# Roots of means between projections: square root on ScalarE and reciprocal on VectorE for logarithm and exponential

## The chip, the cores and the metric

The kernel runs on one core of a Trainium2 chip. The metric is the device time of one execution in microseconds (us), as the median of several runs. TensorE (PE) multiplies matrices, VectorE (DVE), ScalarE (ACT) and GpSimd (POOL) work elementwise, SyncE (SP) issues the transfers.

## The reference, cut to what matters

A first transformer block is followed by a second block of two layers, all in float32, on 512 tokens of width 1024. The change touches the root-mean-square norms that stand between a projection and the next one:

```python
def rms_norm_2(x, g):
    xf = x.astype(jnp.float32)
    y = xf * lax.rsqrt(jnp.mean(xf * xf, axis=-1, keepdims=True) + EPS)
    return (y * g.astype(jnp.float32)).astype(x.dtype)

# second block, each layer l (two layers)
x = x + rms_norm_2(mix, mix_post_g[l])
h = rms_norm_2(x, mem_pre_g[l])
...
x = x + rms_norm_2(memory_cross_attention(h, mem_n, ...), mem_post_g[l])
h = rms_norm_2(x, ffn_pre_g[l])
x = x + rms_norm_2(conv_ffn_2(h, ...), ffn_post_g[l])
```

Between the two blocks, the first block's output is normed once (`norm_final`) and then normed again for the second block.

## The kernel before, in words

Activations lie transposed: 1024 features as 8 tiles (KT) of 128 partitions by 512 tokens. Weights come from memory in slabs of 128 x 2048 through a ring; ACT rounds each slab (L218) and DVE subtracts to get its lower part (L225), and every product is three matmuls (upper by upper, upper by lower, lower by upper). The program is a row of stages, each a block in which every engine has its own instruction list; at the end of a block all engines meet. The two layers of the second block are one hardware loop over the same stages.

A norm needs, for each token, the sum of squares over 1024 features. ACT squares the eight tiles, PE multiplies each by a matrix of ones and adds up in one bank, so that every partition holds the sum, and `root_of_mean` (L510 to L514) turns the 128 x 512 sums into scales: ACT takes the logarithm of mean plus epsilon (L512), drains, and takes the exponential of minus one half of it (L514). That is 1 / sqrt(mean + eps).

A **seam** is what follows a projection in the second block: class `PostNorm` (from L659). It has two roots. Three stages of a layer end with one: `mix_out` and `mem_out` (both `project`, L1475) and the down projection (`ffn_down`, L1405). In order:

- `square` (L683) and `sum` (L689) run while the projection's last tiles are computed. `rms` waits for the last sum and takes the **first root**, signalling `scale_ready`.
- ACT then rounds one slab (`round_second`). In `vector`, DVE waits for `scale_ready`, and for each tile multiplies by gain and scale (L732) and adds the result to the residual `xT` (L737, five tiles; POOL adds the other three, L746). Then DVE halves one slab (`halve_to`, L225).
- ACT squares the new `xT` tiles as they come (`next_squares`, L719), PE sums them (`next_sums`, L697), and `next_rms` takes the **second root**, for the norm with which the next stage begins. It signals nothing: the end of the block is what orders it before the next stage, whose DVE begins with the multiplication by that scale (L623 in `Norms`, with `given=True`).

`final_norm` (L2231), between the blocks, has the same two roots: the first is waited for by DVE (L2267), the second ends the stage. So the function is executed 3 x 2 x 2 + 2 = 14 times. Other norms (`Norms.scalar`, L581 and L583, and L2403 and L2405) have logarithm and exponential of their own.

ACT evaluates functions from a table; the compiler puts a table load (`ACT_TABLE_LOAD`) ahead of an activation whose function is not in the table that is loaded. The profile attributes it to the activation's line. The second block's other functions are the tanh form of GELU (L505 in `in2`, L1364 in the convolution) and the exponentials of softmax (L1077, L1220, L876).

Of the kernel before, what the change touches and what calls it, by code (L numbers as in the profile page):

```python
# [23 lines left out]
ACT = mybir.ActivationFunctionType  # L24
# [3 lines left out]
D = 1024  # L28
# [85 lines left out]
def build_program(nc, stream, xT_in, ctxT_in, memT_in, pos_in, const_in, axial_in, par1_in, par2_in, out):  # L114
    stack = ExitStack()
    with stack:
# [27 lines left out]
        bank = stack.enter_context(nc.psum_tensor("bank", [P, 8, 512], F32))  # L144
        post_gain = small[:, 0:KT]

        def con(name, n=P, at=0):
            return const[:, CONST[name] + at:CONST[name] + at + n]
# [156 lines left out]
        def stage(name, tensor=None, scalar=None, vector=None, gpsimd=None, sync=None):  # L305

            with nc.Block() as block:  # L307
                if tensor:
                    @block.tensor
                    def _(pe):  # L310
                        tensor(pe)

                @block.sync
                def _(sp):
                    if sync:
                        sync(sp)
                    ws.feed(sp, ws.limit)
                if scalar:
                    @block.scalar
                    def _(act):  # L320
                        scalar(act)
                if vector:
                    @block.vector
                    def _(dve):
                        vector(dve)
                if gpsimd:
                    @block.gpsimd
                    def _(pool):
                        gpsimd(pool)
# [179 lines left out]

        def root_of_mean(act, dst, sums):  # L510

            nc.scalar.activation(dst, sums, ACT.Ln, bias=con("eps", 1), scale=1.0 / D)  # L512
            act.drain()  # L513
            return nc.scalar.activation(dst, dst, ACT.Exp, scale=-0.5)  # L514

        class Norms:

# [123 lines left out]
            def gpsimd(self, pool):  # L641
                for k in range(1, 2 * self.halved, 2):
                    j = self.jobs[0]
                    pool.wait_ge(self.upper_ready.sem, self.upper_ready.at(k + 1))
                    nc.gpsimd.tensor_tensor(j["end"][2](k), j["out"](k), j["end"][1](k).bitcast(F32), ALU.subtract)\
                        .then_inc(self.lower_by_pool.sem, 1)
                for n, j in enumerate(self.jobs):
                    if j["end"] and j["end"][0] == "times":
                        for k in range(j["tiles"]):
                            pool.wait_ge(self.normed.sem, self.normed.at(self.starts[n] + k + 1))  # L650
                            nc.gpsimd.tensor_tensor(j["out"](k), j["end"][1](k), j["src"](k), ALU.mult)
# [7 lines left out]
        class PostNorm:  # L659
# [43 lines left out]

            def next_rms(self, act):
                act.wait_ge(self.next_square_summed.sem, self.next_square_summed.at(KT))
                root_of_mean(act, self.next_scale, bank[:, 1, :])

            def next_squares(self, act):
                pool = dve = 0
# [16 lines left out]

            def vector(self, dve, second):
                dve.wait_ge(self.scale_ready.sem, self.scale_ready.at(1))
                for n in range(KT + 1):
                    if n < KT:  # L730
                        src = bank[:, n, :] if n else self.raw[:, 0, :]
                        nc.vector.scalar_tensor_tensor(self.raw[:, n, :], src, self.gain(n), self.scale, ALU.mult, ALU.mult)\  # L732
                            .then_inc(self.normed.sem, 1)
                    if n >= 1 and n - 1 not in self.pool_tiles:

                        dve.wait_ge(self.normed.sem, self.normed.at(n))
                        nc.vector.tensor_tensor(xT[:, n - 1, :], xT[:, n - 1, :], self.raw[:, n - 1, :], ALU.add)\  # L737
                            .then_inc(self.added_by_dve.sem, 1)
                ws.halve_to(dve, second, second + 1)

            pool_tiles = range(0, KT, 3)

# [1025 lines left out]
        def tmp(name, shape, where=None, dt=F32):  # L1768
            return new(where or phase, name, shape, dt)
# [14 lines left out]
        with ExitStack() as here:  # L1784
# [15 lines left out]
            def sync(sp):  # L1800
                sp.dma_start(par1[:, :], par1_in).then_inc(params_in.sem, 16)
                ws.feed(sp, RING)
                sp.dma_start(const[:, :], const_in).then_inc(inputs_loaded.sem, 16)
                sp.dma_start(xT[:, :, :], xT_in).then_inc(inputs_loaded.sem, 16)
                sp.dma_start(pos_i[:, :], pos_in.to_broadcast([P, T])).then_inc(inputs_loaded.sem, 16)
# [21 lines left out]
            def tensor(pe):  # L1827

                def turn(g):
                    pe.wait_ge(rows_ready.sem, rows_ready.at(g + 1))  # L1830
                    for e in range(4):
                        n = 4 * g + e
                        last = nc.tensor.transpose(bank[:, 0, 2 * n:2 * n + 2], rows[:, n * P:(n + 1) * P], con("ident", 2)[0:2, :])
                    return last
                pe.wait_ge(c_ready.sem, c_ready.at(1))
                for g in range(GROUPS):
                    if g >= 4:
                        pe.wait_ge(rows_ready.sem, rows_ready.at(g - 3))
                    for k in range(KT):
                        b = B1_AT["mod"] + (g * KT + k) * 4  # L1840
                        last = ws.mm_whole(pe, b, bank[0:2, 1 + g % 4, :], sc[:, k, :], k == 0, k == KT - 1)
                    last.then_inc(group_done.sem, 1)
                    if g == 2:
                        pe.wait_ge(inputs_loaded.sem, 16 * 3)
                    if g >= 2:
                        turn(g - 2)
                turn(GROUPS - 2)
                turn(GROUPS - 1).then_inc(mod_done.sem, 1)
# [116 lines left out]
        with ExitStack() as s:  # L1965
# [8 lines left out]
            sums = [in_x[:, 0:C_HEADS * ALLT].rearrange("p (n t) -> p n t", n=C_HEADS), tmp("scan_sums", [P, C_HEADS, ALLT], s)]  # L1974
# [246 lines left out]
        scales2 = tmp("scales2", [P, 2, T], phase)  # L2221
# [9 lines left out]
        def final_norm():  # L2231

            squared = Signal("final_squared", 2 * KT)
            summed = Signal("final_summed", 2 * KT)
            normed = Signal("final_normed", KT)
            scale_ready = Signal("final_scale_ready", 1)
            params_loaded = Signal("params_loaded", 16)
            rows = squares2[:, 0:SQUARES, :]

            def sync(sp):  # L2240
                sp.dma_start(par2[:, :], par2_in[0]).then_inc(params_loaded.sem, 16)
                sp.wait_ge(params_loaded.sem, params_loaded.at(16))

            def scalar(act):
                for n in range(2 * KT):
                    if n >= SQUARES:
                        act.wait_ge(summed.sem, summed.at(n - SQUARES + 1))
                    if n >= KT:
                        act.wait_ge(normed.sem, normed.at(n - KT + 1))
                    nc.scalar.activation(rows[:, n % SQUARES, :], xT[:, n % KT, :], ACT.Square).then_inc(squared.sem, 1)  # L2250
                    if n == KT - 1:
                        act.wait_ge(summed.sem, summed.at(KT))
                        root_of_mean(act, scales2[:, 1, :], bank[:, 0, :]).then_inc(scale_ready.sem, 1)
                        ws.round_second(act, RING_SLABS + 1)
                act.wait_ge(summed.sem, summed.at(2 * KT))
                root_of_mean(act, scales2[:, 0, :], bank[:, 1, :])

            def tensor(pe):
                for n in range(2 * KT):
                    pe.wait_ge(squared.sem, squared.at(n + 1))  # L2260
                    nc.tensor.matmul(bank[:, n // KT, :], con("ones"), rows[:, n % SQUARES, :], start=n % KT == 0,
                                     stop=n % KT == KT - 1).then_inc(summed.sem, 1)

            def vector(dve):
                dve.wait_ge(scale_ready.sem, scale_ready.at(1))
                for n in range(KT):
                    nc.vector.scalar_tensor_tensor(xT[:, n, :], xT[:, n, :], p1("norm_final", 1, n), scales2[:, 1, :],  # L2267
                                                   ALU.mult, ALU.mult).then_inc(normed.sem, 1)
                ws.halve_to(dve, RING_SLABS + 1, RING_SLABS + 2)
            stage("norm_final", tensor=tensor, scalar=scalar, vector=vector, sync=sync)  # L2270
        final_norm()

# [427 lines left out]
```

## Time and profile before

| | us |
|---|---|
| median of 3 runs (lowest, highest) | 3588.16 (3587.02, 3592.61) |
| the profiled execution's own time | 3586.33 |
| its span, first to last instruction | 3584.5 |
| PE busy | 3089.6 (86%) |
| DVE busy | 1579.2 (44%) |
| ACT busy | 1337.3 (37%) |
| POOL busy | 555.9 (16%) |
| mean granted TensorE clock, as a share of full speed | 0.918 |

Busy time is the sum of an engine's instructions. PE is the busiest engine over the whole, which says nothing of single stretches: a seam has to be read in the timeline, where each row has its start, its duration, the engine, the line, the tensors and, in brackets, how long the engine had been idle and who ended that.

### The profile page before, as it was taken

What the parts mean: (1) busy time and instruction counts of PE and PEld (TensorE: products, weight loads), DVE (VectorE), ACT (ScalarE), POOL (GpSimd) and SP (SyncE); (2) the same over time, 40 slices, a digit from 0 to 9 for tenths busy, and PEclk for the clock granted to TensorE, in tenths of its full rate; (3) what the DMA queues carried; (4) which work ended last, traced back from release to release, by engine and by line L of the source; (5) the groups of instructions that cost most, each with busy time, mean ns of one, the idle gap of its engine ahead of it and who ended that gap; (6) DMA issues with size and microseconds to landing.
All of it is one profiled execution on the core that took longest, in us unless ns stands there. A gap on an engine that the chain in (4) does not pass through costs nothing. (4 is left out here: it accounts for less than half of the span.)

```text
span 3584.5 us, 40672 instructions
## 1 busy us (share of the span) xinstructions
PE 3089.6 (86%) x15048; PEld 2395.5 (67%) x15048; DVE 1579.2 (44%) x2077; ACT 1337.3 (37%) x1888; POOL 555.9 (16%) x519
## 2 busy tenths in 40 slices
PE   7886788779999999887878889999887788889998
PEld 2775766458877878664456768877664457768875
DVE  2455534336544443335634434442335643444433
ACT  3832224453233332433444333332433443343323
POOL 0144413230000110003301111100104210111100
PEclk8987989799999999998788999999998689999999
DMA  5100021004532222210012212222210022112222
GB/s 207 59 1 0 1 87 36 1 24 154 176 116 94 94 82 94 76 62 24 1 47 82 83 59 94 100 95 83 72 59 1 1 71 106 59 59 100 99 90 83
DMA packets 41485, 253.94 MB, mean 71 GB/s; under 512 B 4592, under 2 KB 4720, under 8 KB 13552
## 3 DMA queue, kind: packets, MB, share of 16 engines
q1 hardware_dynamic: 41328, 251.87, 19.6%
q8 instruction: 96, 1.57, 0.2%
q14 instruction: 61, 0.50, 0.0%
HBM read 249.75 MB, written 2.10 MB: 70 GB/s over the span
## 5 line engine op out<-in xcount | busy, mean ns | idle before, releaser
L225 DVE TENSOR_TENSOR ring_lo<-ring,ring_hi 128x2048 fp32r<-128x2048 f32 x201 | 460.6, 2292 | 913.8 <-ACT ring_hi L218 913.8
L276 PE MATMUL bank<-h_hi,ring_hi 128*128 128x512 f32 x1488 | 613.0, 412 | 111.9 <-DVE ring_lo L225 42.5
L276 PE MATMUL bank<-h_hi,ring_lo 128*128 128x512 f32 x1488 | 590.8, 397 | 0.0
L218 ACT ACTIVATE ring_hi<-ring 128x2048 fp32r<-128x2048 f32 x201 | 383.7, 1909 | 492.2 <-PE bank L276 367.4
L276 PEld LDWEIGHTS bank<-h_hi,ring_hi 128*128 128x128 f32 x1488 | 286.6, 193 | 195.9 <-issue 77.1
L1311 PE MATMUL bank<-h_hi,ring_hi 128*128 128x512 f32 x960 | 374.1, 390 | 5.9 <-DVE ring_lo L225 5.9
L1315 PE MATMUL bank<-h_hi,ring_lo 128*128 128x512 f32 x960 | 373.5, 389 | 0.0
L1314 PE MATMUL bank<-h_lo,ring_hi 128*128 128x512 f32 x960 | 373.5, 389 | 0.0
L276 PEld LDWEIGHTS bank<-h_hi,ring_lo 128*128 128x128 f32 x1488 | 285.8, 192 | 66.7
L276 PE MATMUL bank<-h_lo,ring_hi 128*128 128x512 f32 x560 | 222.3, 397 | 0.0
L276 PE MATMUL bank<-gated_lo,ring_hi 128*128 128x512 f32 x528 | 211.0, 400 | 0.0
L1311 PEld LDWEIGHTS bank<-h_hi,ring_hi 128*128 128x128 f32 x960 | 180.2, 188 | 45.6 <-issue 8.4
L1315 PEld LDWEIGHTS bank<-h_hi,ring_lo 128*128 128x128 f32 x960 | 180.2, 188 | 37.5
L1314 PEld LDWEIGHTS bank<-h_lo,ring_hi 128*128 128x128 f32 x960 | 180.2, 188 | 37.2
L1382 DVE SCALAR_TENSOR_TENSOR mix<-bank,par,mix 128x511 f32<-128x511 f32 x176 | 123.8, 745 | 132.6 <-ACT mix L1359 124.0
L276 PEld LDWEIGHTS bank<-h_lo,ring_hi 128*128 128x128 f32 x560 | 108.3, 193 | 22.4
L1396 POOL TENSOR_TENSOR gated<-mix 128x512 f32 (+1 forms) x44 | 57.0, 1297 | 424.6 <-ACT mix L1364 424.6
L1359 ACT ACTIVATE mix<-bank,par 128x512 f32<-128x512 f32 x88 | 63.7, 774 | 148.9 <-PE bank L1315 148.9
L276 PEld LDWEIGHTS bank<-gated_lo,ring_hi 128*128 128x128 f32 x528 | 100.5, 190 | 24.0 <-issue 2.4
L746 POOL TENSOR_TENSOR xT<-xT,raw 128x512 f32<-128x512 f32 x18 | 27.4, 1525 | 565.0 <-DVE raw L732 565.0
L276 PE MATMUL bank<-mix_lo,ring_hi 128*128 128x512 f32 x256 | 103.4, 404 | 0.0
L386 PE MATMUL bank<-h_hi,ring_hi 128*128 128x512 f32 x160 | 66.5, 416 | 32.8 <-DVE h_lo L636 26.9
(417 smaller groups left out, 5505.7 us busy)
## 6 DMA issues: line engine op xcount, KB each, us to landing
ring<-in_stream SPq DMA_DIRECT2D x210, 1024.0 KB, 4.8
mod_w<-in_stream SPq DMA_DIRECT2D x64, 256.0 KB, 5.1
xT<-in_xT SPq DMA_DIRECT2D x2, 2048.0 KB, 14.2
const<-in_const SPq DMA_DIRECT2D x1, 2306.5 KB, 15.7
par<-in_par SPq DMA_DIRECT2D x3, 696.0 KB, 4.0
memT<-in_memT SPq DMA_DIRECT2D x2, 1024.0 KB, 4.7
out<-xT SPq DMA_DIRECT2D x1, 2048.0 KB, 6.3
ctxT<-in_ctxT SPq DMA_DIRECT2D x1, 1024.0 KB, 4.8
```

The source lines that it names most:

```text
L218: nc.scalar.activation(self.slab_hi(slab + j), self.slab(slab + j), ACT.Copy).then_inc(slab_rounded, 1)
L225: nc.vector.tensor_tensor(lower, self.slab(slab + j), self.slab_hi(slab + j).bitcast(F32), ALU.subtract)\
L276: ins = nc.tensor.matmul(out, lhsT, rhs, start=start and w is w_hi and x is x_hi, stop=stop and w is w_lo)
L386: first = nc.tensor.matmul(out, w_hi, x_hi, start=k == 0, stop=False)
L746: nc.gpsimd.tensor_tensor(xT[:, n, :], xT[:, n, :], self.raw[:, n, :], ALU.add)\
L1311: first = nc.tensor.matmul(out_ap[s], w_hi, x_hi, start=k == 0, stop=False)
L1314: nc.tensor.matmul(out_ap[s], w_hi, x_lo, start=False, stop=False)
L1315: last = nc.tensor.matmul(out_ap[s], w_lo, x_hi, start=False, stop=k == KT - 1)
L1359: last = nc.scalar.activation(work[:, j % 2, s, :], out_ap[s], ACT.Identity, bias=conv_b(col), scale=conv_w(2 * FT + col))
L1382: last = nc.vector.scalar_tensor_tensor(w, out_ap[s][:, 1 - lo:T - lo], conv_w(col), w, ALU.mult, ALU.add)
L1396: nc.gpsimd.tensor_tensor(gated(n), work[:, j % 2, 0, :], work[:, j % 2, 1, :], ALU.mult)\
```

## The change

`root_of_mean` becomes one activation, the square root of mean plus epsilon. DVE takes the reciprocal in place before it uses the scale (first roots), or at the end of its list in the block (second roots); the second roots now signal, and DVE waits for that.

```diff
         def root_of_mean(act, dst, sums):
-            nc.scalar.activation(dst, sums, ACT.Ln, bias=con("eps", 1), scale=1.0 / D)
-            act.drain()
-            return nc.scalar.activation(dst, dst, ACT.Exp, scale=-0.5)
+            return nc.scalar.activation(dst, sums, ACT.Sqrt, bias=con("eps", 1), scale=1.0 / D)
...
             def next_rms(self, act):
                 act.wait_ge(self.next_square_summed.sem, self.next_square_summed.at(KT))
-                root_of_mean(act, self.next_scale, bank[:, 1, :])
+                root_of_mean(act, self.next_scale, bank[:, 1, :]).then_inc(self.next_scale_ready.sem, 1)
...
             def vector(self, dve, second):
                 dve.wait_ge(self.scale_ready.sem, self.scale_ready.at(1))
+                nc.vector.reciprocal(self.scale, self.scale)
+                dve.drain()
                 for n in range(KT + 1):
...
                 ws.halve_to(dve, second, second + 1)
+                dve.wait_ge(self.next_scale_ready.sem, self.next_scale_ready.at(1))
+                nc.vector.reciprocal(self.next_scale, self.next_scale)
```

In `final_norm` the same is done: `scale_ready` counts two, the second root signals it, and DVE's list becomes

```diff
                 dve.wait_ge(scale_ready.sem, scale_ready.at(1))
+                nc.vector.reciprocal(scales2[:, 1, :], scales2[:, 1, :])
+                dve.drain()
                 for n in range(KT):
...
                 ws.halve_to(dve, RING_SLABS + 1, RING_SLABS + 2)
+                dve.wait_ge(scale_ready.sem, scale_ready.at(2))
+                nc.vector.reciprocal(scales2[:, 0, :], scales2[:, 0, :])
```

## Rows read from the trace of the kernel before

**Rows 1.** The profile page, section 1: busy time of each engine.

```profile
PE 3089.6 (86%) x15048; PEld 2395.5 (67%) x15048; DVE 1579.2 (44%) x2077; ACT 1337.3 (37%) x1888; POOL 555.9 (16%) x519
```

**Rows 2.** Chain of waits that ended last (start us, us, what).

```profile
3565.45 9.25 PE bank L697 x16
...
3574.72 0.69 ACT scales L512
...
3575.46 1.28 ACT L514
```

**Rows 3.** Timeline, seam of mix_out, first layer (start us, us, engine, line, operation).

```profile
1873.52 1.28 ACT L512 ACT_TABLE_LOAD   x1
1875.40 0.69 ACT L512 ACTIVATE scales<-bank,const 128x512 f32<-128x512 f32 x1 [0.60 <-PE bank L689]
1876.14 1.28 ACT L514 ACT_TABLE_LOAD   x1
1877.44 0.63 ACT L514 ACTIVATE scales<-scales 128x512 f32<-128x512 f32 x1
...
1878.10 0.75 DVE L732 SCALAR_TENSOR_TENSOR raw<-raw,par,scales 128x512 f32<-128x512 f32 x1 [12.76 <-ACT scales L514]
...
1886.81 2.28 DVE L225 TENSOR_TENSOR ring_lo<-ring,ring_hi 128x2048 fp32r<-128x2048 f32 x1
...
1888.28 1.28 ACT L512 ACT_TABLE_LOAD   x1
1891.07 0.69 ACT L512 ACTIVATE scales<-bank,const 128x512 f32<-128x512 f32 x1 [1.50 <-PE bank L697]
...
1893.10 0.63 ACT L514 ACTIVATE scales<-scales 128x512 f32<-128x512 f32 x1
...
1894.02 2.08 DVE L623 SCALAR_TENSOR_TENSOR hT<-xT,par,scales 128x512 f32<-128x512 f32 x3 [4.93 <-PEq L307]
...
1896.76 0.80 PE L386 MATMUL bank<-h_hi,ring_hi 128*128 128x512 f32 x1 [5.73 <-DVE h_lo L636]
```

**Rows 4.** Groups of ACT instructions by line (busy us, mean ns | idle before).

```profile
L512 ACT ACT_TABLE_LOAD x14 | 18.0, 1283 | 0.3
L514 ACT ACT_TABLE_LOAD x14 | 18.0, 1283 | 0.8
```

**Rows 5.** ACT timeline: the next table load after a seam of each stage.

```profile
1922.80 1.28 ACT L581 ACT_TABLE_LOAD   x1
...
2149.29 1.28 ACT L1364 ACT_TABLE_LOAD   x1
...
2573.33 1.28 ACT L505 ACT_TABLE_LOAD   x1
```

**Rows 6.** DVE timeline, first stage: the one reciprocal of eight elements, and what follows.

```profile
35.21 0.19 DVE L1883 RECIPROCAL scr<-scr 128x8 f32<-128x8 f32 x1
35.48 0.17 DVE L1885 TENSOR_TENSOR scr<-scr 128x8 f32<-128x8 f32 x1
```

**Rows 7.** Single lines: durations in ns, minimum/median/maximum, then first and last start.

```profile
L1883 DVE RECIPROCAL scr<-scr x1: 193/193/193, 35.2 to 35.2; 128x8 f32<-128x8 f32 x1
L1110 DVE RECIPROCAL stat<-stat x32: 165/166/167, 1677.9 to 2782.1; 128x2 f32<-128x2 f32 x32
L1110 DVE RECIPROCAL statB<-statB x16: 153/155/166, 688.1 to 757.6; 128x2 f32<-128x2 f32 x16
L914 DVE RECIPROCAL stat<-stat x32: 162/164/166, 2012.6 to 3096.5; 128x1 f32<-128x1 f32 x32
```

**Rows 8.** Groups of DVE instructions by line and form (busy us, mean ns | idle before).

```profile
L1872 DVE TENSOR_SCALAR ang<-ang 128x512 f32<-128x512 f32 x2 | 0.9, 427 | 0.2
...
L2322 DVE TENSOR_TENSOR hT<-bank,raw 128x512 f32<-128x512 f32 x16 | 10.5, 687 | 9.1 <-PE bank L276 9.1
...
L2375 DVE TENSOR_TENSOR squares<-zv,sgu_stat 128x1024 f32<-128x1024 f32 x2 | 2.5, 1226 | 0.1
```

**Rows 9.** Stretches: length, PE, PEld, DVE, ACT, POOL busy, PE clock, DMA share, GB/s.

```profile
1891.00:1894.00 3.00, 0.03 (x1) 0.00 (x0) 0.00 (x0) 2.60 (x3) 0.00 (x0) 0.96 0.00 0
1894.00:1896.70 2.70, 0.00 (x0) 0.00 (x0) 2.68 (x5) 1.82 (x3) 0.52 (x1) 0.50 0.53 185
1896.70:1900.50 3.80, 3.74 (x9) 2.98 (x10) 3.80 (x5) 1.32 (x3) 2.51 (x2) 0.50 0.75 276
```

More of the change, by code:

```diff
@@ L2235, in final_norm @@
             normed = Signal("final_normed", KT)
-            scale_ready = Signal("final_scale_ready", 1)
+            scale_ready = Signal("final_scale_ready", 2)
             params_loaded = Signal("params_loaded", 16)
@@ L2255, in scalar @@
                 act.wait_ge(summed.sem, summed.at(2 * KT))
-                root_of_mean(act, scales2[:, 0, :], bank[:, 1, :])
+                root_of_mean(act, scales2[:, 0, :], bank[:, 1, :]).then_inc(scale_ready.sem, 1)
             def tensor(pe):
```

## The prediction

> **What bounds the kernel now.** The table of busy time comes first: PE works 86% of the span and DVE 44%, so a change to ACT and DVE can only pay or cost where PE stands still [rows 1]. The chain that ended last shows that the seams are such places: it runs from the sums of squares to the logarithm, a table load and the exponential, with nothing beside them [rows 2]. The timeline of one seam has the detail [rows 3]. The first root: the logarithm starts at 1875.40, the exponential at 1877.44 (it ends at 1878.07), and DVE, idle for 12.76 us, multiplies from 1878.10. The second root: the logarithm starts at 1891.07, the exponential ends at 1893.73, and after the meeting of the engines DVE multiplies from 1894.02; PE gets its first matmul at 1896.76. Both roots lie wholly on the path, since neither PE nor DVE has anything else to do, and the timeline repeats this in the other five seams and in `final_norm`, 14 roots in all.
>
> **What the change removes.** Of the two table loads of a pair (14 on L512 and 14 on L514, 1283 ns each, [rows 4]), the first ends before its logarithm may start: ACT was idle for another 0.60 us at the first root and 1.50 us at the second, waiting for PE's sums [rows 3]. A load there costs nothing, whichever table it brings; with no wait for sums it would cost its 1.28 us. The second load, between logarithm and exponential, is on the path, and so is the exponential. A root now takes 2.70 us from the logarithm's start to DVE's multiplication, or 2.66 us to the exponential's end at the second root.
>
> **What it adds.** The square root has the logarithm's shape, operands and scale, so I take its 0.69 us [rows 3]; the function alone should not change the rate, and a tenth more would be 0.07 us. ACT hands over to DVE in 0.03 us (1878.07 to 1878.10). Then comes the reciprocal, R, and behind the drain 0.08 us until the next instruction, as after the one reciprocal that is followed by a drain (35.21 + 0.19, next at 35.48; [rows 6]). First root: 0.69 + 0.03 + R + 0.08 = R + 0.80, against 2.70: a change of R - 1.90 us. Second root: 0.69 + 0.03 + R = R + 0.72, against 2.66: R - 1.94 us. With seven of each, the sum is 7 (R - 1.90) + 7 (R - 1.94) = 14 R - 26.9 us. It is zero at R = 1.92 us.
>
> **What R is.** No reciprocal of 512 elements is in the trace; there are ones of 1, 2 and 8 [rows 7]. The lower bound is the cheapest DVE pass over 128x512, 0.43 us for a TENSOR_SCALAR; the ordinary pace is 0.69 us for 512 elements and 1.23 us for 1024, which is 1.05 ns per element [rows 8]. The reciprocals grow faster. From 155 ns for two elements (the median of one group) to 193 ns for eight there are 38 ns over six elements, 6.3 ns each. From the other group's 166 ns it is 4.5 ns each, and from 164 ns for one element 4.1 ns each. So R lies between 0.16 + 511 x 4.1 ns = 2.3 us and 0.16 + 510 x 6.3 ns = 3.4 us if this line goes on. I take the upper one, 3.4 us: the shortest two-element reciprocals are the ones least lengthened by something else, and a fixed part that is padded in short instructions hides growth, never invents it. Then the sum is 14 x 3.4 - 26.9 = +20.7 us.
>
> The page "VectorE: DVE Perf Modes" of the Trainium skill, section "First, the fixed hardware budget", speaks against this change: it says that the reciprocal is an iterative divide with a repeat count of 8. What eight passes would give is a rival below.
>
> **Table loads elsewhere.** Up to the next root, squares (L719) and the slab's rounding (L218) run under whatever table is there, so the second square root should need no load, and 28 loads become 7: one for each seam and one for `final_norm`. If it did need one, that lies in the 2.79 us between 1888.28 and 1891.07 in which the old one lies [rows 3]. Leaving the exponential's table costs nothing later: after the three seams of a layer the next functions load a table already, for a logarithm (L581) and for GELU (L1364, L505) [rows 5]. Were one of these new, it would be 1.28 us, six times: 7.7 us.
>
> The rows show no more than the load's 1.28 us between the functions: the load starts at 1876.14 and the exponential 1.30 us later [rows 3]. By the page "ScalarE: Activation LUTs" of the Trainium skill, section "What ACT_TABLE_LOAD costs", a switch is 2.66 us with its drain; by that figure the sum would be 14 x 1.38 = 19.3 us lower, an estimate near zero change. The same page's section "Table sets: the hidden batching unit" says that logarithm and exponential share a set and need one load; this trace has two for each pair, and by the page the change would save no load and the sum would be 18 us higher. The trace contradicts both, and I go by it.
>
> **The rest.** The reciprocal of the second root stands last in DVE's list, behind the halving of the slab, which ends at 1889.09, 2.7 us before the square root would (1891.76): it delays nothing that is queued there [rows 3]. If that slack were gone the slab would hold up the reciprocal. At the first root, all of DVE's multiplications and with them POOL's additions, ACT's squares and PE's sums move by the same R - 1.90. ACT rounds its slab 2 us earlier, for which nobody waits. Transfers issued at the start of the next stage (SP's) move with the meeting of the engines. PE's clock has fallen from 2.4 to 1.2 GHz (granted 0.96, then 0.50) by 1894 already, before the next stage's first matmul, and stays there until about 1900.5 [rows 9]. A longer pause starts as cold; only when it warms can shift, by some fraction of the 3.8 us at half speed in each of seven places, so up to 4 us either way in all. I put this at zero and keep it for the range.
>
> The sum stands against the profiled execution's 3586.3 us, its span of 3584.5 and 1.8 around it; the median of the runs is 1.8 us higher. So 3586.3 + 20.7 = 3607.0 for such an execution and 3608.9 for the median; I say 3608.
>
> **Rivals.** What a measurement of this kernel can tell from no change is about 0.2%, 7.2 us; by the sum that is R under 1.41 us for faster and over 2.44 us for slower.
>
> *The reciprocal streams, faster.* If DVE takes one element per 1.05 ns, as its other operations do [rows 8], R is 0.69 us and the sum 14 x 0.69 - 26.9 = -17.2 us: 3571. It decides at the reciprocal itself, below R = 1.41. For it: the 8-element reciprocal is only 25 ns longer than the TENSOR_TENSOR after it (193 against 168), which could be a fixed extra. Against it: at two elements the extra is nearly absent (155), so it grows [rows 7]. At 0.43 us it would be -20.9 us. Chance 0.10.
>
> *A middle price, no change.* With 4.1 ns per element R is 2.3 us and the sum +5.3 us: 3593. For it: the one- and two-element groups at 164 and 166 ns hold most of the samples. Chance 0.15.
>
> *Eight passes.* R = 0.15 + 512 x 8 x 1.05 ns = 4.45 us, sum +35.4 us: 3624. Against it: from two to eight elements that would add 50 ns, where the rows have 38 at most. Chance 0.14. This is the repeat count of the page "VectorE: DVE Perf Modes" of the Trainium skill, read as passes of the pace in the rows.
>
> *The loads do not go.* If something loads the exponential's table again on the path, or the square root's load comes after the sums, 14 x 1.28 = 17.9 us come on top: 3626. The rows speak against it, since the load on L512 comes ahead of the wait. Chance 0.03.
>
> **How the numbers follow.** My forecast, R between 2.5 and 4 us, has 0.58: slower by 8 to 29 us. Eight passes and loads that stay are slower too, so slower gets 0.75, the middle price gives 0.15 for the same, streaming 0.10 for faster. The range takes in the forecast, eight passes at its upper end, and the middle price less the clock's shift at its lower end: 3592 to 3624. It leaves out streaming and the worst of the rest.
>
> **What would show it.** In the changed kernel's timeline: a group of 14 reciprocals of 128x512, whose mean is R; no table load between the square root and DVE's reciprocal; 7 loads instead of 28; DVE's multiplication R + 0.80 us after the square root's start; the second root's reciprocal last in the block, with the next stage 0.3 us behind it. I would be wrong by the reciprocal's price alone if all else holds: each 0.1 us of R is 1.4 us of time. If the seams lengthen as said and the whole does not, the clock or the start of later stages has given it back.

## The result: 24 us slower, as the price of the reciprocal had it

The changed kernel takes 3614.68 us (median of 4 runs, 3612.18 to 3616.12), the kernel before in the same session 3590.39 us. The ratio is 1.0067, with an interval of 1.005 to 1.0085: slower by 18 to 31 us. Forecast were 3608 us, between 3592 and 3624.

The groups of ACT instructions on the changed line in the profile after (busy us, mean ns, idle before) have 7 table loads where [rows 4] had 28 on the two lines, and no exponential:

```profile
L512 ACT ACTIVATE scales<-bank,const 128x512 f32<-128x512 f32 x14 | 9.6, 688 | 24.3 <-PE bank L695 16.4 <-PE bank L2263 4.3 <-PE bank L687 3.6
L512 ACT ACT_TABLE_LOAD x7 | 9.0, 1283 | 0.1
```

The groups of DVE instructions after have what no row of before could show, the reciprocal of 128x512. All 14 take 3353 ns:

```profile
L727 DVE RECIPROCAL scales<-scales 128x512 f32<-128x512 f32 x6 | 20.1, 3353 | 66.1 <-ACT scales L512 66.1
L741 DVE RECIPROCAL scales<-scales 128x512 f32<-128x512 f32 x6 | 20.1, 3353 | 12.4 <-ACT scales L512 12.4
L2268 DVE RECIPROCAL scales<-scales 128x512 f32<-128x512 f32 x1 | 3.4, 3353 | 8.9 <-ACT scales L512 8.9
L2275 DVE RECIPROCAL scales<-scales 128x512 f32<-128x512 f32 x1 | 3.4, 3353 | 4.3 <-ACT scales L512 4.3
```

The timeline after, of the seam that stands in [rows 3] for before:

```profile
1881.36 1.28 ACT L512 ACT_TABLE_LOAD   x1
1883.25 0.69 ACT L512 ACTIVATE scales<-bank,const 128x512 f32<-128x512 f32 x1 [0.60 <-PE bank L687]
1883.83 1.90 ACT L218 ACTIVATE ring_hi<-ring 128x2048 fp32r<-128x2048 f32 x1
1883.97 3.35 DVE L727 RECIPROCAL scales<-scales 128x512 f32<-128x512 f32 x1 [10.78 <-ACT scales L512]
1887.40 0.75 DVE L732 SCALAR_TENSOR_TENSOR raw<-raw,par,scales 128x512 f32<-128x512 f32 x1
...
1896.12 2.28 DVE L225 TENSOR_TENSOR ring_lo<-ring,ring_hi 128x2048 fp32r<-128x2048 f32 x1
1899.67 0.69 ACT L512 ACTIVATE scales<-bank,const 128x512 f32<-128x512 f32 x1 [2.73 <-PE bank L695]
1900.39 3.35 DVE L741 RECIPROCAL scales<-scales 128x512 f32<-128x512 f32 x1 [1.99 <-ACT scales L512]
...
1904.05 2.08 DVE L621 SCALAR_TENSOR_TENSOR hT<-xT,par,scales 128x512 f32<-128x512 f32 x3 [0.30 <-PEq L307]
...
1906.78 0.79 PE L386 MATMUL bank<-h_hi,ring_hi 128*128 128x512 f32 x1 [7.15 <-DVE h_lo L634]
```

From the square root's start to the multiplication there are now 4.15 us, against 2.70 us; from the second square root to the next stage's first multiplication 4.38 us, against 2.95 us. The first table load is where it was, 0.60 us ahead of the wait's end; at the second root there is none, and ACT waits 2.73 us for PE instead of 1.50. And the chain that ended last goes through DVE now:

```profile
3602.46 0.70 ACT scales L512
3603.16 0.02 issue
3603.18 3.35 DVE scales L741
```

The profiled spans differ by more than the medians, 3614.3 - 3584.5 = 29.8 us. Cut at the roots, with all seven seams of each trace measured like the one above:

| part of the span | before, us | after, us | difference |
|---|---|---|---|
| start to the first root (nothing changed there) | 1464.4 | 1467.8 | +3.3 |
| seven first roots, to DVE's multiplication | 18.9 | 29.1 | +10.2 |
| multiplication to second root, seven times | 86.5 | 85.2 | -1.3 |
| six second roots, to the next stage's multiplication | 21.7 | 30.4 | +8.6 |
| six stretches from there to the next first root | 1983.2 | 1990.0 | +6.9 |
| last second root to the end | 9.8 | 11.8 | +2.1 |

The roots are as forecast. What is over is in code that the change does not touch. The 3.3 us is scatter of the start: over all traces of this document that part, the same code in each, takes 1461 to 1470 us. Of the last 2.1 us, 1.4 are the second root and some 0.7 belong to the final transfer (7.0 us to landing against 6.3). The 6.9 us between the seams was not forecast, and much of what follows is about it. A good part of it can be read in these two traces already, where PE restarts behind a second root, with its first matmul of the next stage. For before, the last row of [rows 9] shows it. After (columns as there):

```profile
1906.78:1911.70 4.92, 4.92 (x12) 3.86 (x13) 4.92 (x5) 1.57 (x4) 2.75 (x2) 0.50 0.79 305
1911.70:1914.00 2.30, 2.30 (x11) 1.94 (x10) 2.30 (x3) 0.97 (x2) 1.66 (x1) 0.95 0.08 32
```

PE works at the 1.2 GHz level for 5.1 us here, where it was 3.8 us before. In the first 8 us of the six restarts behind a second root, added up, the low clock takes 30.2 us against 19.4. At half speed the 10.8 us more are up to 5.4 us of time, an estimate; that would be most of the 6.9.

### The profile page after: what moved, and what is told of

It reads as the page before. It is cut to its first block and busy times, and to the rows that moved or that the text cites. A ratio compares the mean times of both kernels' runs of the same rounds, so it can differ in the third digit from the quotient of the medians.

```text
span 3614.3 us, 40650 instructions
## 1 busy us (share of the span) xinstructions
PE 3095.5 (86%) x15048; PEld 2400.3 (66%) x15048; DVE 1626.3 (45%) x2091; ACT 1302.5 (36%) x1853; POOL 556.4 (15%) x519
```

## Experiments

All are compared with the kernel before, run beside them. "Rows" is what the roots' own rows in that kernel's profile add up to.

### The changed kernel again, and each kind of root alone

> The changed kernel once more, beside the kernel before in the same session. Theory A, the reciprocal's price alone: 14 x 3.35 us less 26.9 us is +20.0 us. Theory B, each seam costs more than its two reciprocals because PE starts the next stage cold for longer after the longer pause: +24 to +30 us. Theory C, the 10 us between the sum and the two profiled spans are the scatter of executions: between +17 and +23 us here, and the stretch before the first root differs as much as anything behind it.

Measured: ratio 1.0062 (1.0049 to 1.0075), so +22 us; the difference of the medians is +23.7. Its rows at the roots are those above, and the stretches between the seams add up to 1990.5 us. The interval, +18 to +27 us, holds A, most of C and the lower part of B, so the time does not decide between them. The two profiles of this kernel agree within 0.5 us between the seams, which speaks against C's scatter there; but of the kernel before there is a single profile, so how far its 1983.2 us would scatter is not shown.

The kernel with first roots alone leaves the second ones as they were:

```diff
             def next_rms(self, act):
...
-                root_of_mean(act, self.next_scale, bank[:, 1, :]).then_inc(self.next_scale_ready.sem, 1)
+                root_of_mean_old(act, self.next_scale, bank[:, 1, :]).then_inc(self.next_scale_ready.sem, 1)
...
-                dve.wait_ge(self.next_scale_ready.sem, self.next_scale_ready.at(1))
-                nc.vector.reciprocal(self.next_scale, self.next_scale)
```

(`root_of_mean_old` is logarithm and exponential; the same in `final_norm`, and mirrored for the kernel with second roots alone.)

> Only the first roots are changed, the second ones are logarithm and exponential as before. A: 7 x (3.35 - 1.90) = +10.2 us. B: the first root lengthens a pause after which PE only adds up squares, which wait for DVE anyway, so +10 us here and the excess is all with the second roots. Rival to both: the loads of the first root's tables had been needed by the second, so a load comes onto the path and it is +19 us.

> Only the second roots are changed. A: 7 x (3.35 - 1.94) = +9.9 us. B: the pause before the next stage's first matmul lengthens from 5.7 us to about 7.2 us and the stretch at 1.2 GHz behind it lengthens too, so +13 to +18 us. C: +10 us give or take 4.

Measured: first roots alone 1.0000 (0.9991 to 1.0008), +0 us where all theories said +10 or more; second roots alone 1.0033 (1.0020 to 1.0046), +12 us. For the second the interval is +7 to +17 us, which holds A and most of B; its six restarts have 30.5 us of low clock, against 19.4 before. The first is a miss, and not at the root. Timeline of the kernel with first roots alone, the seam of [rows 3]:

```profile
1873.34 0.69 ACT L512 ACTIVATE scales<-bank,const 128x512 f32<-128x512 f32 x1 [0.60 <-PE bank L693]
1874.06 3.35 DVE L733 RECIPROCAL scales<-scales 128x512 f32<-128x512 f32 x1 [10.78 <-ACT scales L512]
1877.49 0.75 DVE L738 SCALAR_TENSOR_TENSOR raw<-raw,par,scales 128x512 f32<-128x512 f32 x1
```

The root takes its 4.15 us here too. Some of the time comes back behind it: the stretch from the start of `mem_qkv` to the last sum of `mem_out` (the mem stretch) takes 209.05 and 208.93 us in the two layers, against 211.98 and 211.93 before. The stretches show why. Before, 5 us each, about 150 to 165 us into that stretch (columns as in [rows 9]):

```profile
2044.00:2049.00 5.00, 4.58 (x36) 4.18 (x36) 1.70 (x7) 1.12 (x4) 0.61 (x1) 1.00 0.00 0
2049.00:2054.00 5.00, 2.20 (x5) 1.82 (x6) 4.04 (x7) 3.69 (x8) 0.00 (x0) 0.68 0.03 7
2054.00:2059.00 5.00, 5.00 (x16) 3.86 (x16) 4.17 (x5) 2.38 (x3) 0.00 (x0) 0.64 0.53 206
```

and the same work with first roots alone:

```profile
2042.70:2047.70 5.00, 4.30 (x36) 3.92 (x35) 1.72 (x7) 1.12 (x4) 0.61 (x1) 1.00 0.00 0
2047.70:2052.70 5.00, 2.50 (x11) 2.06 (x12) 4.04 (x7) 4.00 (x8) 0.00 (x0) 1.00 0.20 29
2052.70:2057.70 5.00, 5.00 (x23) 4.05 (x22) 4.45 (x5) 2.69 (x3) 0.00 (x0) 1.00 0.44 184
```

PE is idle for some 3 us in the middle 5 in both, between the last matmul of the attention over the memory and the first of `mem_out` (3.19 us before, 3.20 us here). Before, its granted clock fell to the 1.2 GHz level and it did 16 matmuls in the 5 us after; here it kept 2.4 GHz and did 23. Added up over this stretch, the granted clock stood low for 30.4 us before and 20.5 us here. So the same short pause, 150 us after the seam, costs PE's speed in one kernel and not in the other, and the seam only moved its start. No other edit of this document keeps that speed: the pause takes 3.2 to 3.5 us in every trace, and the mean clock of the 5 us after it is 1.00 with first roots alone and 0.50 to 0.72 in all the others. Nor does it repeat in each kernel. The changed kernel's first mem stretch takes 211.1 us in the profile of the table above and 213.1 us in the next one, where before has 212.0; so this pause is not where the 6.9 us of the table come from.

### The price of load and exponential, and of the reciprocal by size

```diff
-                nc.vector.reciprocal(self.scale, self.scale)
+                nc.vector.tensor_scalar(self.scale, self.scale, 0.02, None, ALU.min)
```

(at all four places)

> The changed kernel with the cheapest pass (minimum with a constant, 128x512 in place) where the reciprocals stand; so the reciprocals are left out. A: R falls from 3.35 to 0.43 us, the sum is 14 x 0.43 - 26.9 = -20.9 us against the kernel before, 41 us under the changed one. This is what the removal of load and exponential is worth by itself. Rival: the load and the exponential were not wholly on the path, then less than 12 us are gained against before.

Measured: 0.9952 (0.9937 to 0.9967), -17 us; rows -20.9 us (the first roots at 1.22 us, the second at 1.45 us up to the next stage's multiplication, the pass at 426 ns). The interval is -23 to -12 us, so the rival's 12 us is not far from its edge; it is the rows that show load and exponential wholly on the path. With a DVE pass at DVE's ordinary price this change would have been the gain of 0.5% that the first rival described.

```diff
-                nc.vector.reciprocal(self.scale, self.scale)
+                nc.vector.reciprocal(self.scale[:, 0:256], self.scale[:, 0:256])
+                nc.vector.tensor_scalar(self.scale[:, 256:512], self.scale[:, 256:512], 0.02, None, ALU.min)
```

(at all four places)

> Reciprocal of 256 of the 512 columns, the cheap pass for the other 256 (their reciprocals are left out). If the price is 6.3 ns per element on 0.15 us fixed, the reciprocal takes 1.75 us and the two passes some 2.0 us: 14 x 2.0 - 26.9 = +1 us against before. Rival, a price that hangs little on the size: about 3 us and +15 us or more.

Measured: 1.0009 (0.9999 to 1.0018), +3 us. The timeline of this kernel:

```profile
1875.68 1.75 DVE L727 RECIPROCAL scales<-scales 128x256 f32<-128x256 f32 x1 [10.78 <-ACT scales L512]
1877.35 0.23 DVE L728 TENSOR_SCALAR scales<-scales 128x256 f32<-128x256 f32 x1
1877.66 0.75 DVE L733 SCALAR_TENSOR_TENSOR raw<-raw,par,scales 128x512 f32<-128x512 f32 x1
```

The group's mean for 256 elements is 1753 ns. With 3353 ns for 512 the line through the two is 1600 / 256 = 6.25 ns per element on 153 ns fixed. The two passes together take 1.9 us, and the root is 2.70 us again: the break-even that the prediction put at R = 1.92 us.

```diff
                 nc.vector.reciprocal(self.scale, self.scale)
+                dve.drain()
+                nc.vector.reciprocal(self.scale, self.scale)
+                dve.drain()
+                nc.vector.reciprocal(self.scale, self.scale)
```

(at all four places)

> Three reciprocals in a row with drains between them where the changed kernel has one. A: R is 3 x 3.35 + 2 x 0.08 = 10.2 us, +115.9 us against before, so 95.9 us over the changed kernel's sum. B: nothing further, since PE's clock is down at each restart already; if the clock's share grows with the pause it is above +125 us.

Measured: 1.0334 (1.0318 to 1.0350), +119.9 us; rows +116.1 us. Three times the pause adds 3.8 us to the rows' sum and one reciprocal adds 2 to 4. The interval, +114 to +126 us, only just reaches B's bound, and the profile speaks against a share that grows with the pause: each root takes 11.0 us instead of 4.15, yet the stretches between the seams take 1989.5 us (changed kernel: 1990.0) and the six restarts have 28.9 us of low clock (changed kernel: 30.2).

### Hidden loads

```diff
-            return nc.scalar.activation(dst, sums, ACT.Sqrt, bias=con("eps", 1), scale=1.0 / D)
+            root = nc.scalar.activation(dst, sums, ACT.Sqrt, bias=con("eps", 1), scale=1.0 / D)
+            nc.scalar.activation(lam_s[:, 7:8], con("one", 1), ACT.Exp)
+            return root
```

> The changed kernel with a one-element exponential on ACT right behind each square root, so that the exponential's table is loaded beside DVE's reciprocal and the square root's table again ahead of each second root: 28 loads instead of 7. A: all 21 added loads are hidden, by the 3.35 us reciprocal and by the 2.7 us that ACT waits for the sums, so the time is the changed kernel's within 2 us. Rival: a load costs its 1.28 us wherever it stands, +27 us over the changed kernel.

Measured: 1.0065 (1.0051 to 1.0079), +23 us, the same as without the 21 loads. The trace of this kernel has all 28, 14 on each of the two lines, and each of the 14 ahead of a square root ends 0.5 to 1.5 us before PE's last sum releases ACT. One seam:

```profile
1878.94 0.69 ACT L512 ACTIVATE scales<-bank,const 128x512 f32<-128x512 f32 x1 [0.60 <-PE bank L689]
1879.65 1.28 ACT L513 ACT_TABLE_LOAD   x1
1880.94 0.20 ACT L513 ACTIVATE lam_s<-const 128x1 f32<-128x1 f32 x1
...
1892.65 1.28 ACT L512 ACT_TABLE_LOAD   x1
1895.37 0.69 ACT L512 ACTIVATE scales<-bank,const 128x512 f32<-128x512 f32 x1 [1.44 <-PE bank L697]
```

In the kernel before, too, the 14 loads ahead of the logarithm all end 0.6 to 1.5 us before ACT is released. So of its 28 loads only the 14 between logarithm and exponential cost anything, and the fall from 28 to 7 overstates what was removed.

### One function in place of two

```diff
-            nc.scalar.activation(dst, sums, ACT.Ln, bias=con("eps", 1), scale=1.0 / D)
-            act.drain()
-            return nc.scalar.activation(dst, dst, ACT.Exp, scale=-0.5)
+            return nc.scalar.activation(dst, sums, ACT.Abs_reciprocal_sqrt, bias=con("eps", 1), scale=1.0 / D)
```

> The kernel before with one activation in place of logarithm and exponential, the function that gives 1 / sqrt(|x|) directly, and no reciprocal. First root 0.69 + 0.03 us against 2.70, second 0.69 against 2.66: 7 x 1.98 + 7 x 1.97 = 27.7 us less than the kernel before, about 3561 us in a session where that takes 3588. If its table were loaded on the path each time it would be 27.7 - 14 x 1.28 = 9.8 us less. B adds: shorter pauses keep PE's clock up in some seams, up to 5 us more gain.

Measured: 0.9905 (0.9890 to 0.9919), -34 us; median 3555.98 us against 3590.13. This kernel beats both the kernel before and the changed one. It has 7 table loads too. Its timeline:

```profile
1877.04 1.28 ACT L512 ACT_TABLE_LOAD   x1
1878.92 0.69 ACT L512 ACTIVATE scales<-bank,const 128x512 f32<-128x512 f32 x1 [0.60 <-PE bank L687]
1879.64 0.75 DVE L730 SCALAR_TENSOR_TENSOR raw<-raw,par,scales 128x512 f32<-128x512 f32 x1 [10.78 <-ACT scales L512]
...
1891.33 0.69 ACT L512 ACTIVATE scales<-bank,const 128x512 f32<-128x512 f32 x1 [2.16 <-PE bank L695]
1892.32 2.08 DVE L621 SCALAR_TENSOR_TENSOR hT<-xT,par,scales 128x512 f32<-128x512 f32 x3 [1.68 <-PEq L307]
```

The root is 0.72 us instead of 2.70, and PE's pause before the next stage is shorter. Rows -27.7 us, just outside the interval of -39 to -29 us. In this profile the seven pieces from multiplication to second root add up to 80.1 us against 86.5, a further 6.4 us: PE's granted clock is low for 17.1 us of them, against 47.8 before. So here a shorter pause does keep the clock up. The rest does not add up as well, since this profile is of the slowest of the four runs (3564.43 us) and has 6 us more between the seams and 6 us more at the start. How accurate this function is by itself was not measured.

### Is the rest alignment?

Theory D came from the first session: where the clock falls in the stages between the seams depends on when these start, and so the same edit at the roots is given back, or paid for, elsewhere. Four more runs, the first a repetition.

> The kernel with the first roots alone changed, once more. Its first roots took 7 x 1.45 = +10.2 us, and the whole +0.0 us; the profiled execution had 10.6 us fewer at full length elsewhere. Theory D: where PE's clock falls and rises in the stages between the seams depends on when they start, so this kernel has an alignment of its own that gives 10 us back, and it comes again: 0 us, give or take 3. Theory E: it was scatter of that session: +10 us.

Measured: 1.0000 (0.9991 to 1.0008) again. The mem stretch took 208.99 and 208.92 us, the clock stood low in it for 20.5 and 20.4 us. E is out: this kernel again costs nothing, and its mem stretch repeats in both layers and both sessions. (The expectation's 10.6 us does not come out of the traces: outside the first roots, the first profile of this kernel is 8.7 us shorter than the one before.)

```diff
                 nc.vector.reciprocal(self.scale, self.scale)
                 dve.drain()
+                nc.vector.tensor_scalar(self.scale, self.scale, 1e9, None, ALU.min)
+                dve.drain()
```

(first roots alone; the same pass ahead of the multiplications in the two kernels after it)

> The same with one more cheap pass and drain (0.5 us) behind each of the seven first reciprocals. If times add up, it is 3.5 us over the kernel with the first roots alone. D: the later start can cost the favourable alignment, so up to 10 us more than that on top, and the seams' own rows still show 0.5 us each.

> The kernel before, untouched but for one cheap pass and drain (0.5 us) ahead of DVE's multiplications at each of the seven first roots. If times add up: +3.5 us. D: anywhere from -6 to +10 us, with the rows at the roots at +0.5 us each, and the lengths of the stretches between the seams changed by as much as the rest.

> The kernel with one function (1 / sqrt directly), with the same 0.5 us pass at each of the seven first roots. If times add up: 3.5 us over that kernel, so about -30.5 us against before, where its own sum of rows was -27.7 us and it measured -34. D: between -34 and -24 us.

| kernel | rows, us | ratio (interval) | measured, us | between the seams, us |
|---|---|---|---|---|
| before | 0 | | 0 | 1983.2 |
| before, with pass | +3.5 | 1.0011 (1.0002 to 1.0020) | +4 | 1988.6 |
| first roots | +10.2 | 1.0000 (0.9991 to 1.0008) | 0 | 1979.8, 1977.7 |
| first roots, with pass | +13.9 | 1.0011 (1.0001 to 1.0020) | +4 | 1982.1 |
| second roots | +9.9 | 1.0033 (1.0020 to 1.0046) | +12 | 1988.8 |
| changed kernel | +20.1 | 1.0062 (1.0049 to 1.0075) | +22 | 1990.5 |
| one function | -27.7 | 0.9905 (0.9890 to 0.9919) | -34 | 1989.3 |
| one function, with pass | -24.2 | 0.9925 (0.9913 to 0.9937) | -27 | 1988.2 |

With the pass, the mem stretch of the kernel with first roots alone went from 209.0 to 211.6 us in both layers, at the place shown above, this time half slow:

```profile
2051.90:2056.90 5.00, 1.80 (x8) 1.34 (x7) 3.57 (x5) 3.01 (x6) 0.00 (x0) 0.91 0.00 0
2056.90:2061.90 5.00, 5.00 (x18) 3.95 (x17) 4.46 (x6) 3.07 (x4) 0.00 (x0) 0.75 0.63 213
```

So it is shown that a seam's edit can change the clock behind a later pause, and D's large jumps are not shown: the three passes moved the totals by 4, 4 and 7 us where 3.5 were in the rows, and each of these is within what the intervals allow. A kernel with a different pause does not get longer stages in proportion (one function, with the shortest pauses, has 1989.3 us; before has 1983.2). The restarts say the same: before with the pass leaves the second roots and the pauses behind them as they were, and its six restarts are at the low clock for 26.7 us against 19.4. The last column is from single profiles and can't be set against the medians within some 5 us: the profiled run of before lies 2.4 us under the median of its 29 runs beside these kernels, the one with the pass 2.4 us over its own. But it goes with the clock: between the seams the low level was granted for 316 us before, 336 and 335 us in the changed kernel, and 307 and 297 us with first roots alone. In full, the residual of rows against measurement runs from -10 us (first roots) to +4 us (three reciprocals). For first roots, the rows behind the root give back 5.5 us of the 10 in one profile and 8.0 in the other (stretches and sums together). The remainder is 4.7 and 2.2 us; the second is inside the interval of 3 us each way, the first is not, and stays open. Why an alignment falls one way for a given kernel was not settled.

## Why the prediction was right

**The path.** Both roots were on the path at full length, seven of each: the rows moved by 1.45 us and 1.43 us where the formulas R - 1.90 and R - 1.94 give 1.45 and 1.41 with the measured R.

**The reciprocal.** The step that carried the forecast was R = 3.4 us, and it measured 3.353 us. The slope of 6.3 ns per element was right within 1%, but partly by luck: on the measured line (153 ns and 6.25 ns per element) two elements would take 166 ns and eight 203 ns. The first is the group I took for the lengthened one, and the eight-element row, 193 ns, lies 10 ns under the line. Taken through the 166 ns group the same extrapolation gave 4.5 ns and R near 2.5 us. Rows of eight elements could bound the price and tell it from one pass, but not fix it within a third.

**The rivals.** Streaming at one element per 1.05 ns failed at the reciprocal itself, by a factor of six; with a pass of 0.43 us in its place, the rival's -20.9 us for that price came true within the interval. The middle price was refuted by the same row. Eight passes would be 8.4 ns per element; it is 6.25, or six intervals of 1.05 ns. The page "VectorE: DVE Perf Modes" of the Trainium skill, section "First, the fixed hardware budget", gives a repeat count of 8. It gives no time, and no run here shows what the operation does inside; my reading of it as eight passes at 1.05 ns, an estimate, is a third above the measured price.

**Loads.** Seven loads, none new in later stages, none between the square root and the reciprocal, as forecast. That a load ahead of the wait costs nothing was shown by adding 21. No drain of a microsecond stands behind a load between logarithm and exponential: all 14 exponentials start 1.3 us after its start. The 2.66 us per switch of the page "ScalarE: Activation LUTs" of the Trainium skill, section "What ACT_TABLE_LOAD costs", would have made the removal worth 19 us more, by the prediction's estimate; with the cheap pass the gain was 17 us, where the rows had 20.9 and that figure would have had 40.

**The clock.** This is the term that was mis-sized. I put it at zero, up to 4 us either way, and took it for a matter of the warm-up behind each restart. For this kernel the place was right: the six restarts are at the low clock for 30.2 and 29.4 us in its two profiles against 19.4 before, up to 5.4 us by half speed, and without the start the profiles are some 6 us over the sum. By the ratios and medians it is +2 to +4 us, and as the sum's +20.0 us lies inside every interval, the times alone do not tell it from zero. It does not go by the length of the pause: three reciprocals leave it at 28.9 us, and before with the pass, whose pauses behind the second roots are unchanged, has 26.7 us. With first roots alone the rest was -10 us, beyond my bound, and it came partly from the pause between attention and `mem_out`, 150 us after the seam, which the prediction did not look at.

**The range.** Its lower end does not follow from the terms it names: 5.3 us for the middle price less 4 us for the clock gives 3588 to 3590 us, not 3592. The measured time lies in the upper half, so nothing hung on it.

**The sum.** 14 x 3.353 - 26.9 = +20.0 us stood against +24.3, +23.7 and +24.1 us in the medians of the three sessions that had these roots.

## What to carry to other kernels

Before trading two ACT functions for one and a DVE reciprocal, price the reciprocal at its size: here 6.25 ns per element of the free axis, six times an ordinary DVE pass, with a break-even of 1.9 us for a table load and an exponential. Count only those table loads that stand between a wait's end and its consumer. Where a change of a few microseconds shifts later stages, add up the rows at the edit and judge the edit by them. In this kernel the total differed from them by up to 10 us, and in the traces part of that was PE's clock, low for longer or shorter behind the same pauses.

## What was not expected of the hardware

The reciprocal takes 1753 ns for 256 and 3353 ns for 512 elements, with a spread of 1 ns. The line through these two gives 203 ns for eight, where the row has 193, so it is nearly but not exactly linear down to there. One activation function gives 1 / sqrt directly at the square root's 688 ns. And whether a pause of PE of about 3 us lowers its clock differs between kernels that do the same work there. With first roots alone it repeats across layers and sessions (20.5, 20.5, 20.5 and 20.4 us of low clock in the mem stretch); in the changed kernel it does not (28.4 us in one profile's first layer, 31.8 us in the other's).
